# Both gathers of a thin and a wide block issued ahead of the scatter of the wide block before them, in a mixture-of-experts stage

## The reference, cut to what matters

```python
x_rows = jnp.concatenate([xt, jnp.zeros((1, D), xt.dtype)], axis=0)[row_tok]   # gather

def expert_block(args):
    xb, e = args
    gt = jnp.minimum(xb @ w_gate[e] + b_gate[e], SWIGLU_LIMIT)
    up = jnp.clip(xb @ w_up[e] + b_up[e], -SWIGLU_LIMIT, SWIGLU_LIMIT)
    hid = gt * jax.nn.sigmoid(SWIGLU_ALPHA * gt) * (up + 1.0)
    return hid @ w_down[e] + b_down[e]

out = jnp.zeros((T + 1, D), x.dtype).at[row_tok].add(y_rows * row_gate[:, None])[:T]   # scatter
```

## Time and profile before

| | |
|---|---|
| median of three runs | 3267.39 us |
| the profiled execution | 3266.21 us |
| its span (first to last instruction) | 3264.5 us |
| PE busy | 2972.8 us (91%) |
| DVE, ACT, POOL busy | 2197.7, 1446.2, 552.4 us |
| mean DMA rate over the span | 259 GB/s |

### The profile page before, as it was taken

How to read it: one execution, slowest core, us unless ns; L and a number is a source line. 1 busy time by engine, 2 the same in 40 slices (tenths; PEclk the granted TensorE clock), 3 DMA queues, 4 the chain that set the end, 5 groups by cost and what they waited for, 6 DMA issues and landing times. The chain is left out here.

```text
span 3264.5 us, 46229 instructions
## 1 busy us (share of the span) xinstructions
PE 2972.8 (91%) x16534; PEld 2451.3 (75%) x16534; DVE 2197.7 (67%) x3585; ACT 1446.2 (44%) x1989; POOL 552.4 (17%) x483
## 2 busy tenths in 40 slices
PE   8999899999999999999998996878888888888888
PEld 7996779999988888888887775555555655555566
DVE  7998736985958888888886557444445555554467
ACT  4455523345953333333333453433444444444355
POOL 0000005451003232322221001111111111111111
PEclk9999899999999999999999997998999999999999
DMA  5320303444569999999985145898898888888895
GB/s 145 84 78 27 130 26 116 145 153 168 221 260 376 350 338 346 347 338 346 347 332 200 53 164 193 329 355 353 327 353 355 355 349 352 353 357 342 337 366 213
DMA packets 192683, 846.93 MB, mean 259 GB/s; under 512 B 20047, under 2 KB 101583, under 8 KB 148992
## 3 DMA queue, kind: packets, MB, share of 16 engines
q1 hardware_dynamic: 165600, 694.50, 55.4%
q0 software_dynamic: 26976, 151.03, 13.1%
HBM read 798.79 MB, written 56.62 MB: 262 GB/s over the span
## 5 line engine op out<-in xcount | busy, mean ns | idle before, releaser
L3611 DVE TENSOR_TENSOR moe_w_lo<-all_raw,moe_w_hi 128x2048 fp32r<-128x2048 f32 x178 | 402.7, 2286 | 114.6 <-ACT moe_w_hi L3494 114.4
L3494 ACT ACTIVATE moe_w_hi<-all_raw 128x2048 fp32r<-128x2048 f32 x178 | 336.2, 1915 | 61.6 <-DMA all_raw<-in_w_moe 44.2
L1984 ACT ACTIVATE experts_wu_hi<-all_wu 128x1024 fp32r<-128x1024 f32 x128 | 135.7, 1060 | 250.7 <-PE experts_Y L1936 241.6
L1330 POOL TENSOR_TENSOR score_w_lo<-all_hT,score_w_hi 128x1024 fp32r<-128x1024 f32 x59 | 146.1, 2478 | 582.4 <-DVE all_x_lo L1479 458.4
L1904 POOL DMA_INDIRECT experts_pair<-in_peer_pairs,experts_slot x128 | 144.2, 1126 | 554.4 <-DVE all_h L2088 542.3
L3383 PE MATMUL moe_GU<-moe_w_hi,moe_x_hi 128*128 128x512 f32 x576 | 225.7, 392 | 0.0
L3384 PE MATMUL moe_GU<-moe_w_lo,moe_x_hi 128*128 128x512 f32 x576 | 225.5, 391 | 0.0
L3385 PE MATMUL moe_GU<-moe_w_hi,moe_x_lo 128*128 128x512 f32 x576 | 225.2, 391 | 0.0
L2062 DVE TENSOR_TENSOR experts_wu_lo<-all_wu,experts_wu_hi 128x1024 fp32r<-128x1024 f32 x128 | 156.8, 1225 | 61.8 <-ACT experts_wu_hi L1984 59.7
L3347 PE MATMUL moe_X<-all_ident,all_mixT 128*128 128x128 f32 x264 | 49.1, 348 | 140.3 <-DMA all_mixT<-h_rows,moe_source 133.0
L3423 PE MATMUL moe_GU<-all_raw,moe_x_thin 128*64 128x256 f32 x1440 | 173.6, 396 | 0.0
(11 more groups left out here) (626 smaller groups left out, 7920.0 us busy)
## 6 DMA issues: line engine op xcount, KB each, us to landing
all_raw<-in_w_moe SPq DMA_DIRECT2D x149, 2048.0 KB, 10.6
all_hT<-in_w_moe SPq DMA_DIRECT2D x49, 2048.0 KB, 12.0
all_wu<-in_peer_pairs SPq DMA_DIRECT2D x64, 1024.0 KB, 7.4
all_hT<-in_peer_wdT SPq DMA_DIRECT2D x122, 512.0 KB, 9.7
peer_gates<-gates_out SPq DMA_DIRECT2D x6, 4096.0 KB, 12.2
experts_gt<-peer_gates SPq DMA_DIRECT2D x32, 768.0 KB, 9.3
all_hT<-in_w_in SPq DMA_DIRECT2D x40, 512.0 KB, 3.8
all_hid<-peer_early SPq DMA_DIRECT2D x60, 192.0 KB, 5.0
```

The lines of the kernel that those rows point to most:

```text
L3494: act.activation(w_hi[p % RING][:], piece_of(r, p), ACT.Copy).then_inc(w_high, 1)
L3611: dve.tensor_tensor(w_lo[p % RING][:], piece_of(r, p), w_hi[p % RING][:].bitcast(F32), ALU.subtract).then_inc(w_low, 1)
```

## The change

Inside the 15 pairs POOL now issues both gathers in a row, the thin block's and the next wide block's, once the wide block's rows are turned. Then come the wide block's scatter and the thin block's. The wait for the thin block's turned rows falls away. Each gather still has its own buffer and its own semaphore. The tail's order is as it was. No other engine's program is changed.

```diff
-                def wide_block(j, u, next_rows):
+                def turned_x(j):
                     pool.wait_ge(x_done, j + 1)
                     pool.sem_inc(paced, 1)
-                    gather(j + 1, 1 - u, next_rows)
+
+                def wide_rows(j, u):
                     file_slots(j, u, 3)
                     scatter(y[:, u, :], slot[:, u, 0:1]).then_inc(stored, 16)
 
-                def thin_block(j):
-                    pool.wait_ge(x_done, j + 1)
-                    pool.sem_inc(paced, 1)
-                    gather(j + 1, 0)
+                def thin_rows_out(j):
                     file_slots(j, 1, 4)
...
                 with pool.Fori(0, PAIRED_BLOCKS) as i:
-                    wide_block(i * 2, 0, HALF_ROWS)
-                    thin_block(i * 2 + 1)
+                    turned_x(i * 2)
+                    gather(i * 2 + 1, 1, HALF_ROWS)
+                    gather(i * 2 + 2, 0)
+                    wide_rows(i * 2, 0)
+                    thin_rows_out(i * 2 + 1)
```

More of the change, by code:

```diff
@@ L3314, in tail_block @@
                         with pool.If(j + 1 < n):
-                            wide_block(j, u, P)
+                            turned_x(j)
+                            gather(j + 1, 1 - u)
+                            wide_rows(j, u)
                         if u == 0:
```

## The result

The changed kernel takes 3131.81 us (3130.20 to 3134.09, 4 runs) against 3267.91 us for the kernel before in the same measurement. That is 136.1 us less, a ratio of 0.9584 with a 95% interval of 0.9567 to 0.9600. The forecast was 3149, its own range 3130 to 3174, the whole range 3124 to 3195.

What follows compares the result with a forecast made beforehand. PE's wait for the late wide gather was taken as the bound, as far as weights could come earlier: 8.5 - 0.6 = 7.9 us per pair, 15 x 7.9 = 118.5 us off, 3149 us; own range 3130 to 3174, whole 3124 to 3195.

Steps and rivals of the forecast that it cites:

- a sign of being wrong: Start of the wide blocks: a dip of PE's clock there would speak against the forecast; no size given.
- The wait: PE's thin block: the transpose's wait for the wide gather goes, 8.87 us on average, 8.33 in the pair followed.
- The low clock: PE's thin block: transposes and the thin chunk behind them run at full clock again, 1.7 us less per pair.
- The new wait: Ahead of the wide block: PE waits 2.1 us for wide chunk 0's weights, starting 8.2 us earlier than before.
- The wide block itself: Wide block up to its result: ends 8.5 us earlier per pair, with PE the later of two at chunk 2.
- PE's pace: Wide block: PE takes 12.8 us from chunk 0 to chunk 2 as before, so it gets there 8.5 us earlier.
- the chain: Wide block: its result comes 32.2 us behind the landing of chunk 2, which was to come 9.8 us earlier.
- The gather in the wide block: Wide block's weight loads: the gather shares their queue and costs 0 to 1.2 us per pair, taken as 0.6.
- The queue as a ceiling: DMA queue: busy 66.1 us of each 75.1 us pair, so never idle would give at most 9.0 us.
- the queue does not pack: Rival, DMA queue: the hole closes but the gather's 1.2 us and small dips stay; 5.0 us per pair, 3192; chance 0.20.
- The clock: Rival, wide block's start: a 2.1 us wait lowers PE's clock, costing 4.0 us per pair; 3209; chance 0.04.
- Slower: Rival, wide block: the gather delays its weights, ending it 2.9 us later per pair; 3310; chance 0.03.

Runs made afterwards that it cites:

- The turn behind chunk 3: The kernel before, with PE's transposes of the next wide rows behind thin chunk 3 instead of chunk 1, POOL's order unchanged: 3149.64 us, ratio 0.9635.
- the fill: The changed kernel plus 9 unread 128x512 matmuls on PE while it waits at the start of a paired wide block: 3133.11 us, ratio 0.9582.
- the gather of 16 rows: The changed kernel, but the wide gather inside the loop reads 16 rows instead of 128: 3134.99 us, ratio 0.9596.
- the later gather: The changed kernel, but POOL waits for the thin rows to be turned before issuing the wide gather, still ahead of the wide scatter: 3129.82 us, ratio 0.9573.
- half a chunk less: The changed kernel, but only half of wide chunk 4 is loaded in the paired blocks: 3122.52 us, ratio 0.9555.

## Why the prediction was right, and where its sum was off

The main line came as forecast: the gather's wait goes, PE's low clock behind it goes too, the landing of wide chunk 0 then becomes what PE waits for, and the gain is what the weights can come earlier. The turn behind chunk 3 shows from another side that the time hung on PE's wait and not on the gather itself. The sum said 7.9 us per pair, and 9.09 were measured. One thing that the prediction named as a sign of being wrong did come: the clock dips at the start of the wide blocks.

- **The wait.** 133.0 us gone, all of it. Right.
- **The low clock.** Transposes 1.97 to 1.09 us (the 1.03 us of the earlier trace rows was that of a thin block's rows, which are turned elsewhere), the chunk behind 4.36 to 3.62, and the bias matmuls between them 1.12 to 0.65, which the forecast left out. In the means this is 7.07 - 5.06 = 2.0 us per pair, forecast 1.7.
- **The new wait.** 2.94 us per pair, forecast 2.1. The forecast took the 8.33 us wait of one pair where the mean was 8.87, and 1.7 us of clock where it was 2.0; these two make up the 0.84 us. Before, PE waited 0.42 us here on average. The start of the wide block thus came 8.87 + 2.0 - 2.94 + 0.42 = 8.4 us earlier (8.44 in the table), where the forecast had 8.2.
- **The wide block itself.** This term was mis-sized. The sum let PE be the later of two at chunk 2 and kept the rest of the block as long as before, which gave 8.5 us, 0.3 of them inside the block. Measured, the block is 0.65 us shorter, although PE comes to chunk 2 later than before (13.0 us behind the start, against 12.5) because of the clock. Chunk 2 landed 8.44 + 6.89 - 5.56 = 9.8 us earlier, just as forecast, but from there to the result it now takes 0.68 us more. So neither row alone gave the right length: the one of PE's pace (8.5) was too low, the one of the chain (9.8) too high. That PE's pace is not what the block hangs on is shown by the fill, which brought PE to chunk 2 1.5 us sooner and left the time as it was. Part of what the block lost are waits inside it, which I had taken as fixed; the kernel before had these two beside the 13.9 us of the earlier trace rows:

```profile
...
PE moe_GU L3354 <- DVE all_row L3639: 11.8, 30, 0.9
PE moe_Y L3393 <- DVE moe_hid_lo L3644: 9.7, 15, 0.7
...
```

Together 35.4 us, of which 9.2 us are left (4.6 and 4.6).
- **The gather in the wide block.** 0.6 us forecast; the gather of 16 rows and the later gather both show nothing. This is the largest part of the miss: 0.6 + 0.35 (inside the block) + 0.24 (its start) = 1.19 us per pair, 18 us in all.
- **The queue as a ceiling.** Never idle was to give 9.0 us per pair; it gave 9.09, at a share of 0.98. The engines were busy 0.98 x 66.0 = 64.7 us per pair, a little less than the 66.1 us from which I took the ceiling, so it was no hard one. Nor was the share a proof that the volume was the limit: half a chunk less, 2.4 us per pair, gave only 9.3 us in all. That the gain came out at the ceiling is luck of the number, then, and not its proof.

Of the rivals, *the queue does not pack* fell by the share. *The clock* did fall behind the new wait: in 13 of 15 pairs the first wide chunk took 7.2 us or more, in the other two 5.8. The rival put 4.0 us per pair on this. Its price was nil, as the fill shows; and the two pairs without it took 66.2 and 66.5 us, no less than the mean of 66.0. *Slower* had the right fear in the wrong place: the same gather costs 1.25 us per pair beside the last thin chunks, and both gathers 2.2 us half a thin block earlier ((3005.47 - 2050.05) / 14 = 68.24), but nothing behind chunk 2. The prediction took from the Trainium skill, "DMA: Bandwidth & Descriptors" (Issuing engines are not separate DMA queues), that DMAs from SP and from GpSimd run on the same 16 engines and interleave. The trace after agrees: with the wide gather under way beside weight chunks, from 2343.24 to 2358.04, the share was 1.01 at 400 GB/s. The ceiling that I worked out from the share held only as a number.

## What to carry to other kernels

When one engine waits for a small transfer, look at what that engine's progress releases: here the loads of the next block, and the DMA queue ran dry behind it. Without the wait of 8.9 us PE was some 10.9 us ahead, and the weights let it keep 8.4 of them. A small transfer beside a full queue costs by its place: put it where nobody waits for the chunks behind it, not simply as early as its buffer allows. And where the profile offers two lengths for a stretch (an engine's pace, and the distance from a landing to the end along the chain), neither needs to hold once the rest has moved. Read both in every pass of the loop and not in one: the wide block of the pair followed here became 1.6 us shorter, the mean 0.65.

## What the hardware showed that was not expected

The wide gather of 0.52 MB took 11.38 us to land beside two weight chunks, and 14.8 us at the start of the wide block behind the thin gather. At 429 GB/s its bytes are 1.2 us. What it cost the kernel per pair was about that, 1.25 us, beside the last thin chunks, and nothing that can be measured behind wide chunk 2: time to landing says little about cost. And a wait of PE of 2.6 to 3.8 us was followed by a slow first chunk, that is a lower clock, in 13 of 15 pairs. The length of the wait alone does not decide it: the two pairs without the fall (granted clock 1.00 over the first chunk) had waits of 2.56 and 3.05 us, and another wait of 2.56 us was followed by one. The 8.33 us wait before had a longer low stretch, partly within it (0.64, 0.50 and 0.84 from 2425 to 2440, against 0.66 from 2335 to 2340).
